# Hybrid decoder step: output projection and second norm interleaved with the MLP of the group before

## The chip, the cores and the metric

The kernel runs on all 8 cores of one Trainium2 chip, two dies of four cores. Every core runs the same program on its own share of the batch. The metric is device time in microseconds of the slowest core. TensorE (PE) does the matmuls, VectorE (DVE) and ScalarE (ACT) the elementwise work, GpSimd (POOL) a little at the start, and SyncE (SP) issues every DMA from one in-order queue.

## The reference, cut to what matters

```python
def _layer(h, ...):
    xn = _rmsnorm(h, ln_mix)
    zq, zf, zi, zg, sq, sk, sv = _split(xn @ w_in)
    o_hg, S_new = _hgrn2(zq, zf, zi, zg, lb, hg_norm, S0)     # linear recurrence, 4 heads of 128
    o_swa = _swa_prompt(q, k, v, sinks)                       # window 128, 8 query heads, 2 kv heads
    h = h + jnp.concatenate([o_hg, o_swa], axis=-1) @ w_out
    u = _rmsnorm(h, ln_mlp) @ w_up
    h = h + jnp.square(jax.nn.relu(u)) @ w_down
    return h, S_new, k_buf, v_buf
y = _rmsnorm(h, ln_final)
```

The model width is 1024, the MLP width 4096. Each core has one prompt sequence of 4096 tokens and 16 decoding sequences of 8 tokens each (128 tokens, the "sample"), with their recurrent states and key/value caches.

## The kernel before, in words

The prompt's 4096 tokens are 32 tiles of 128 tokens, worked in 8 groups of four. For a group the tile of activations is kept transposed, 8 blocks of 128 features by 512 tokens: xnT (normed x), omT (mixer output), hnT (normed h), aT (MLP activation). The residual stream XR has 8 slots of one token tile, so two groups.

The weights are 24 chunks of 1024 x 512. Chunks 0 to 5 are the input projection, 6 and 7 the output projection, 8 to 15 w_up, 16 to 23 w_down. A ring of five slots (s_wr) holds them in bf16. At its first use a chunk comes as fp32 in four quarters to s_stg, is cast by ScalarE and VectorE in turns (L337 to L350) and stored to wbf in HBM; from then on it is read from there. `w_release` frees a slot and issues the next chunk's load; `w_use` puts the pending casts into the engines' queues. Ten chunks are cast before and during the sample's own mixer, the other 14 after it.

Work is written as generators that yield after each step, and the order in which a step is emitted is its order in each engine's in-order queue:

- `head12_steps`: first norm of four tiles (`norm_pre`: statistics on ScalarE, L457 to L461, scale on VectorE to s_xnb, L468; `norm_post`: 8 transposes, L475, and a copy, L477), then the input projection (`fm_mm` L486, `tm_mm` L493), the gates of the recurrence (L540 to L562), and keys and values.
- `p3_tile_steps`: the mixer of one tile in nine steps. Recurrence: L611, L619, L663 to L669, norm L637. Window attention: scores L716, exp L720, mask multiply L723, values L742 and denominators L743, and `swa_finish` (four adds L694, a reciprocal L699, a multiply into omT L707).
- `p45`: for each tile two output matmul groups (L898, 8 matmuls each), the add into XR (L902), `norm_pre`, and, two tiles late, `norm_post` into hnT.
- `mlp_steps`: four rounds of 8 up groups (L486 on hnT; relu L928, square into aT L931) and 8 down groups (L939, add into XR L943). One group is 8 matmuls.
- `p8`: final norm (L457, L960) and the store of y.

Each phase allocates one of 8 PSUM banks per group, in the order in which banks came free. A wait is set by whole buffers: any write to hnT must be done before a matmul that reads any part of it.

The main loop for group g loads x for g+1, runs `p45(g)` by itself, then takes one step of `mlp_steps(g)` and one of the front half of g+1 (`head12_steps`, then the mixer) in turns until both are done, then `p8(g)`. Ahead of the loop the sample's `p45` and MLP are taken in turns with the front half of group 0; this is where the 14 chunks are cast.

The softmax here doesn't subtract the row's maximum and nothing guards it: scores larger than these inputs give would overflow.

## Time and profile before

| | us |
|---|---|
| median of 3 runs (2219.98 to 2221.53) | 2221.41 |
| span of the profiled execution, slowest core | 2217.1 |
| spans of the eight cores | 2200.3 to 2217.1 |
| TensorE busy | 1667.9 (75%) |
| ScalarE busy | 931.1 (42%) |
| VectorE busy | 864.2 (39%) |

Of the profiled execution the profile gives the span alone, from the first to the last instruction of the slowest core; its own time as the runs are timed is not given. The median of the runs is 4.3 us over that span. A busy TensorE is not TensorE at full rate: its granted clock is shown beside it, and matmuls at half the clock count as busy for twice as long. Line numbers are those of the kernel before.

### The profile page before, as it was taken

What the parts mean: (1) busy time and instruction counts of PE and PEld (TensorE: products, weight loads), DVE (VectorE), ACT (ScalarE), POOL (GpSimd) and SP (SyncE); (2) the same over time, 40 slices, a digit from 0 to 9 for tenths busy, and PEclk for the clock granted to TensorE, in tenths of its full rate; (3) what the DMA queues carried; (4) which work ended last, traced back from release to release, by engine and by line L of the source; (5) the groups of instructions that cost most, each with busy time, mean ns of one, the idle gap of its engine ahead of it and who ended that gap; (6) DMA issues with size and microseconds to landing.
All of it is one profiled execution on the core that took longest, in us unless ns stands there. A gap on an engine that the chain in (4) does not pass through costs nothing.

```text
span 2217.1 us, 26417 instructions; the slowest of 8 cores (2200.3 to 2217.1 us)
## 1 busy us (share of the span) xinstructions
PE 1667.9 (75%) x8533; PEld 773.3 (35%) x8533; DVE 864.2 (39%) x1438; ACT 931.1 (42%) x1861; POOL 28.6 (1%) x59
## 2 busy tenths in 40 slices
PE   0301354345999699969996999699969996999797
PEld 0201232212443244334433443344334443443343
DVE  1113413144245624561356235523652355235412
ACT  1312334242446344544454454444444444444433
POOL 2001000000000000000000000000000000000000
PEclk9755586766999899989998999899989998999899
DMA  7774476760242434343424342434334333442332
GB/s 193 229 223 142 142 247 233 272 226 32 102 171 99 168 106 161 114 152 125 147 108 152 133 152 98 149 133 152 114 133 152 135 113 133 152 155 95 128 143 76
DMA packets 77767, 326.66 MB, mean 147 GB/s; under 512 B 7584, under 2 KB 29088, under 8 KB 49952
## 3 DMA queue, kind: packets, MB, share of 16 engines
q1 hardware_dynamic: 77632, 324.97, 42.6%
q8 instruction: 71, 1.16, 0.2%
q14 instruction: 64, 0.52, 0.1%
HBM read 277.76 MB, written 49.15 MB: 147 GB/s over the span
## 4 chain that ended last, share of the span: by engine, by line
PE 59%; DMA 11%; DVE 10%; ACT 9%; issue 6%; SPq 2%; POOL 0%; ACTq 0%; DVEq 0%; POOLq 0%
PE pb L486 27%; PE pb L939 19%; DMA s_stg<-wall 9%; PE pb L898 4%; PE pb L493 3%; DVE U L699 3%; ACT s_junk L457 3%; SPq L103 2%; PE pb L742 2%; DMA XR<-st 2%; DVE XR L902 2%; PE pb L716 1%; ACT s_rl L928 1%; PE pb L743 1%; ACT U L720 1%
## 5 line engine op out<-in xcount | busy, mean ns | idle before, releaser
L939 PE MATMUL pb<-s_wr,s_aT 128*128 128x512 bf16 x2112 | 497.3, 382 | 88.3 <-ACT s_aT L931 29.1
L486 PE MATMUL pb<-s_hnT,s_wr 128*128 128x512 bf16 (+1 forms) x2304 | 507.1, 369 | 17.5 <-ACT s_rl L928 8.0
L943 DVE TENSOR_TENSOR XR<-pb,XR 128x512 f32<-128x512 f32 x264 | 182.2, 690 | 557.0 <-PE pb L939 555.2
L939 PEld LDWEIGHTS pb<-s_wr,s_aT 128*128 128x128 bf16 x2112 | 199.8, 98 | 333.4 <-issue 119.3
L486 PEld LDWEIGHTS pb<-s_hnT,s_wr 128*128 128x128 bf16 x2304 | 214.7, 100 | 264.0 <-issue 49.9
L486 PE MATMUL pb<-s_xnT,s_wr 128*128 128x512 bf16 (+1 forms) x1224 | 274.2, 373 | 19.8 <-ACT U L521 9.6
L928 ACT ACTIVATE s_rl<-pb 128x512 bf16<-128x512 f32 (+1 forms) x288 | 160.2, 556 | 198.1 <-PE pb L486 197.9
L931 ACT ACTIVATE s_aT<-s_rl 128x512 bf16<-128x512 bf16 (+1 forms) x288 | 171.6, 596 | 27.0 <-ACT s_rl L928 0.7
L898 PE MATMUL pb<-s_wr,s_omT 128*128 128x512 bf16 x528 | 141.5, 435 | 52.0 <-DVE s_omT L707 46.0
L486 PEld LDWEIGHTS pb<-s_xnT,s_wr 128*128 128x128 bf16 x1224 | 120.3, 103 | 148.8 <-issue 25.3
L457 ACT ACTIVATE s_junk<-XR 128x1024 bf16<-128x1024 f32 x99 | 103.8, 1048 | 160.5 <-DVE XR L902 134.0
L475 PE MATMUL pb<-s_ident,s_xnb 128*128 128x128 bf16 x528 | 49.2, 255 | 149.5 <-DVE s_xnb L468 149.3
L699 DVE RECIPROCAL U<-U 128x512 f32<-128x512 f32 x33 | 110.6, 3353 | 3.4
L720 ACT ACTIVATE U<-pb 128x512 bf16<-128x512 f32 x128 | 75.6, 591 | 85.5 <-PE pb L716 85.5
L493 PE MATMUL pb<-s_wr,s_xnT 128*128 128x256 bf16 (+1 forms) x528 | 100.1, 334 | 9.5 <-ACT U L532 9.5
L898 PEld LDWEIGHTS pb<-s_wr,s_omT 128*128 128x128 bf16 x528 | 56.5, 109 | 136.1 <-issue 92.1
L475 PEld LDWEIGHTS pb<-s_ident,s_xnb 128*128 128x128 bf16 x528 | 41.2, 115 | 162.3 <-issue 156.3
L468 DVE TENSOR_SCALAR s_xnb<-XR,s_rs 128x1024 bf16<-128x1024 f32 x66 | 49.6, 752 | 115.6 <-ACT s_rs L461 115.6
L742 PE MATMUL pb<-U,s_vS_all 128*64 128x512 bf16 x126 | 54.1, 429 | 43.4 <-DVE U L723 43.3
L621 ACT COPY U<-pb 128x512 bf16<-128x512 bf16 x33 | 19.2, 582 | 141.0 <-PE pb L619 141.0
L723 DVE TENSOR_TENSOR U<-U,s_swm_cur 128x512 bf16<-128x512 bf16 x64 | 27.2, 426 | 117.9 <-ACT U L720 117.9
L493 PEld LDWEIGHTS pb<-s_wr,s_xnT 128*128 128x128 bf16 x528 | 52.3, 100 | 51.4 <-issue 13.7
(140 smaller groups left out, 1349.0 us busy)
## 6 DMA issues: line engine op xcount, KB each, us to landing
s_wr<-wbf SPq DMA_DIRECT2D x192, 1024.0 KB, 4.9
s_stg<-wall SPq DMA_DIRECT2D x96, 512.0 KB, 8.7
wbf<-s_wr SPq DMA_DIRECT2D x24, 1024.0 KB, 4.8
XR<-x SPq DMA_DIRECT2D x32, 512.0 KB, 6.0
y<-XR SPq DMA_DIRECT2D x32, 512.0 KB, 4.1
XR<-st SPq DMA_DIRECT2D x16, 256.0 KB, 3.2
ss<-XR SPq DMA_DIRECT2D x16, 256.0 KB, 2.6
XR<-ck SPq DMA_DIRECT2D x4, 256.0 KB, 4.1
```

The costliest lines, as they stand in the source:

```text
L457: P.op("act", lambda e: e.activation(out=junk[:, :], in_=src[:, :], func=AF.Square, accum_out=ssq[:, 0:1]), reads=[src], writes=[ssq, junk])
L475: P.op("pe", [lambda e, k=k: e.transpose(bkb[:, k * 128:(k + 1) * 128], xb[:, k * 128:(k + 1) * 128], C.ident[:, :]) for k in range(8)], r ...
L486: P.op("pe", [lambda e, k=k: e.matmul(bk[0:ncols, 0:TB], lhsT=W[:, k, col0:col0 + ncols], rhs=srcT[:, k, 0:TB], start=(k == 0), stop=(k == ...
L493: P.op("pe", [lambda e, k=k: e.matmul(bk[:, 0:ncols], lhsT=srcT[:, k, j * 128:(j + 1) * 128], rhs=W[:, k, 0:ncols], start=(k == 0), stop=( ...
L699: P.op("dve", lambda e: e.reciprocal(out=B.rden[:, :], in_=B.dsum[:, :]), reads=[B.dsum], writes=[B.rden])
L720: P.op("act", lambda e: e.activation(out=pt[:, :], in_=bkS[:, :], func=AF.Exp, scale=0.125), reads=[bkS], writes=[pt])
L742: P.op("pe", [lambda e: e.matmul(swO[rows, :], lhsT=vS_all[:, ks, rows], rhs=pt[:, :], start=first, stop=last), lambda e: e.matmul(swD[row ...
L898: P.op("pe", [lambda e, k=k, W=W, bk=bk: e.matmul(bk[:, :], lhsT=omT[:, k, j * 128:(j + 1) * 128], rhs=W[:, k, :], start=(k == 0), stop=(k ...
L928: P.op("act", lambda e, bk=bk, rl=rl: e.activation(out=rl[:, 0:TB], in_=bk[:, 0:TB], func=AF.Relu), reads=[bk], writes=[rl])
L931: P.op("act", lambda e, fl=fl, rl=rl: e.activation(out=aT[:, fl, 0:TB], in_=rl[:, 0:TB], func=AF.Square), reads=[rl], writes=[aT])
L939: P.op("pe", [lambda e, f=f, W=W, j=j, bk=bk: e.matmul(bk[:, :], lhsT=aT[:, f, j * 128:(j + 1) * 128], rhs=W[:, f, :], start=(f == 0), sto ...
L943: P.op("dve", lambda e, nh=nh, bk=bk, xs_=xs_: e.tensor_tensor(out=xs_[:, nh * 512:(nh + 1) * 512], in0=bk[:, :], in1=xs_[:, nh * 512:(nh ...
```

## The change

The output projection and the second norm leave their own phase. `p45` goes. `back_steps` takes the mixer of a group's tiles and, after the third and the sixth step of tile j, one output group of tile j-1 each; the transposes of the second norm follow behind the next output group. All of it belongs to the front half, which runs beside the MLP of the group before, so hnT gets a second buffer (taken from the space of the DMA scratch). x for group g+2 is loaded when the MLP of g ends. `p8` of a tile follows its last down group.

The two halves no longer take turns one by one. Each step yields a weight; a first build sums them, and `interleave` keeps the two sums in proportion, after 6 steps of the MLP alone. In the front half the chunks come in the order 2, 0, 1, 3, 4, 5, and each gate step stands ahead of one group of chunk 3. The transposed tiles are tracked by token tile (xnT, hnT, omT) or by feature row (aT), and a down group is issued in three parts (6, 1 and 1 matmuls), each with its own wait.

```diff
+W_DENSE = 0.25
+W_ATT = 1.2
+W_OUT = 0.6
+W_WAIT = 3.0
+PACE = 1.04
+LEAD = 6
...
-    nc = bass.Bass("TRN2", target_bir_lowering=False)
+    nc = bass.Bass("TRN2", target_bir_lowering=False, dynamic_dma_scratch_size=1024)
...
-    xnT = sb("xnT", [8, 512], BF16)
-    hnT = sb("hnT", [8, 512], BF16)
+    class Cols:
+        __slots__ = ("ap", "t")
...
+            if cut == "cols":
+                self.t = [Buf(self.ap[:, :, j * 128:(j + 1) * 128]) for j in range(n // 128)]
+            else:
+                self.t = [Buf(self.ap[:, k, :]) for k in range(8)]
...
+    xnT = Cols("xnT", 512, "cols")
+    hnTs = [Cols("hnT%d" % i, 512, "cols") for i in range(2)]
...
-    omT = sb("omT", [8, 512], BF16)
-    aT = sb("aT", [8, 512], BF16)
+    omT = Cols("omT", 512, "cols")
+    aT = Cols("aT", 512, "rows")
...
-             reads=[W, srcT], writes=[bk])
+             reads=[W] + srcT.t[0:TB // 128], writes=[bk])
...
+            xbs.append(norm_pre(slots[j]))
+            if j < 2:
+                yield W_WAIT
+            if j >= 1:
+                norm_post(xbs[j - 1], xnT, j - 1)
+                yield W_OUT
+        yield W_OUT
+        norm_post(xbs[nt - 1], xnT, nt - 1)
+        yield W_DENSE
+        W, u = w_use(2)
...
+        for cid, dst in ((0, B.qtT), (1, B.sgT)):
+            W, u = w_use(cid)
...
         W, u = w_use(3)
         for g in range(4):
+            gate(g)
             bk = fm_mm(W, g * 128, xnT, TB)
...
+    def back_steps(B, tiles, slots, hn):
+        pend = []
+
+        def post():
+            if pend:
+                xb0, j0 = pend.pop(0)
+                norm_post(xb0, hn, j0)
+
+        def out_tile(Ws, j):
+            for nh, W in enumerate(Ws):
+                out_mm(W, nh, j, slots[j])
+                if nh == 0:
+                    post()
+                yield W_OUT
+            pend.append((norm_pre(slots[j]), j))
+
+        Ws = None
+        prev = iter(())
         for j, n in enumerate(tiles):
-            for _ in p3_tile_steps(B, j, n):
-                yield
-        if tiles[-1] == NT - 1:
-            for h in range(4):
-                final_toks.append(P.dma(sp_d[h], S[h].ap, reads=[S[h]], sem="spo"))
+            for i, w in enumerate(p3_tile_steps(B, j, n)):
+                yield w
+                if j > 0 and i in (2, 5):
+                    if Ws is None:
+                        (W6, u6), (W7, u7) = w_use(6), w_use(7)
+                        Ws = (W6, W7)
+                    if i == 2:
+                        prev = out_tile(Ws, j - 1)
+                    w = next(prev, None)
+                    if w is not None:
+                        yield w
+            for w in prev:
+                yield w
+            if j == len(tiles) - 1:
+                yield W_WAIT
+            if n == NT - 1:
+                for h in range(4):
+                    final_toks.append(P.dma(sp_d[h], S[h].ap, reads=[S[h]], sem="spo"))
+        for w in out_tile(Ws, len(tiles) - 1):
+            yield w
+        w_release(u6)
+        w_release(u7)
+        while pend:
+            yield W_WAIT
+            post()
...
-    def p45(B, slots):
...
+    def out_mm(W, nh, j, xs_):
+        bk = psum()
+        P.op("pe", [lambda e, k=k: e.matmul(bk[:, :], lhsT=omT[:, k, j * 128:(j + 1) * 128], rhs=W[:, k, :],
+                                            start=(k == 0), stop=(k == 7)) for k in range(8)],
+             reads=[omT.t[j], W], writes=[bk])
+        P.op("dve", lambda e: e.tensor_tensor(out=xs_[:, nh * 512:(nh + 1) * 512], in0=bk[:, :],
+                                              in1=xs_[:, nh * 512:(nh + 1) * 512], op=ALU.add), reads=[bk], writes=[xs_])
+        pfree(bk)
...
+                    for fa, fb in ((0, 6), (6, 7), (7, 8)):
+                        P.op("pe", [lambda e, f=f: e.matmul(bk[:, :], lhsT=aT[:, f, j * 128:(j + 1) * 128], rhs=W[:, f, :],
+                                                            start=(f == 0), stop=(f == 7)) for f in range(fa, fb)],
+                             reads=aT.t[fa:fb] + [W], writes=[bk])
...
+                    if q == 3 and nh == 1:
+                        p8(slots[j], ydst[j * 128:(j + 1) * 128, :])
+                    yield 1.0
...
+    def interleave(key, genA, genB, lead):
+        done = {"a": 0.0, "b": 0.0}
+        total = (weights or {}).get(key, {"a": 1.0, "b": 1.0})
+        ok = {"a": True, "b": True}
+
+        def step(which, gen):
+            w = next(gen, None)
+            if w is None:
+                ok[which] = False
+            else:
+                done[which] += w
+
+        for _ in range(lead):
+            step("a", genA)
+        a0 = done["a"]
+        while ok["a"] or ok["b"]:
+            fa = (done["a"] - a0) / max(1e-6, total["a"] - a0)
+            fb = done["b"] / max(1e-6, total["b"])
+            if ok["b"] and (fb <= fa * PACE or not ok["a"]):
+                step("b", genB)
+            else:
+                step("a", genA)
+        wsum[key] = done
...
+            p45_sample(Bs, xsmp, hnTs[1])
+            yield 1.0
+            for w in mlp_steps(Bs, [xsmp], hnTs[1], ys_d):
+                yield w
+
+        def front(g):
+            slots = [xload[n] for n in gtiles(g)]
+            return chain(head12_steps(Bp, gtiles(g), slots, False), back_steps(Bp, gtiles(g), slots, hnTs[g % 2]))
+
+        interleave("s", sample_tail(), front(0), 0)
...
+        for n in gtiles(1):
+            load_x(n)
...
+            genA = mlp_steps(Bp, [xload[n] for n in gtiles(g)], hnTs[g % 2], y_d[g * G * 128:(g + 1) * G * 128, :])
+            interleave(g, genA, front(g + 1) if g + 1 < NG else iter(()), LEAD if g + 1 < NG else 0)
+            if g + 2 < NG:
...
-            xb_last = p45(Bp, slots)
-            genA = mlp_steps(Bp, slots, xb_last)
-            if g + 1 < NG:
-                nslots = [xload[n] for n in gtiles(g + 1)]
-                genB = chain(head12_steps(Bp, gtiles(g + 1), nslots, False), head3_steps(Bp, gtiles(g + 1)))
-                interleave(genA, genB)
-            else:
-                drain(genA)
-            p8(slots, y_d[g * G * 128:(g + 1) * G * 128, :])
...
+    _, _, steps = build_program()
+    _, order, _ = build_program(weights=steps)
+    nc, _, _ = build_program(worder=order, weights=steps)
```

TensorE at the end of a group's mixer, before (L716, L742, L743: attention; L898: output projection; L475: transposes of the norms; L486 on s_hnT: the next MLP):

```order
L716 MATMUL pb<-U,s_kT_all 128x512
L742 MATMUL pb<-U,s_vS_all 64x512
L743 MATMUL pb<-U,s_ones 64x512
L898 MATMUL pb<-s_wr,s_omT 128x512 x48
L475 MATMUL pb<-s_ident,s_xnb 128x128 x8
L898 MATMUL pb<-s_wr,s_omT 128x512 x16
L475 MATMUL pb<-s_ident,s_xnb 128x128 x40
L486 MATMUL pb<-s_hnT,s_wr 128x512 x8
```

The same place in the changed kernel (L754, L755: attention; L506: up groups; L979: down groups; L941: output projection; L495: transposes):

```order
L754 MATMUL pb<-U,s_vS_all 64x512
L755 MATMUL pb<-U,s_ones 64x512
L506 MATMUL pb<-s_hnT,s_wr 128x512 x16
L979 MATMUL pb<-s_wr,s_aT 128x512 x24
L941 MATMUL pb<-s_wr,s_omT 128x512 x8
L495 MATMUL pb<-s_ident,s_xnb 128x128 x8
L941 MATMUL pb<-s_wr,s_omT 128x512 x8
L979 MATMUL pb<-s_wr,s_aT 128x512 x24
L495 MATMUL pb<-s_ident,s_xnb 128x128 x8
L979 MATMUL pb<-s_wr,s_aT 128x512 x16
L506 MATMUL pb<-s_hnT,s_wr 128x512 x64
```

The block of 64 output matmuls is gone; its last two groups stand between down groups of the preceding MLP, and 64 up matmuls of the next group follow without front work.

ScalarE late in the weight stream, before (L337, L347: casts of a chunk; L584: keys; L928, L931: relu and square of the sample's MLP):

```order
L337 ACTIVATE s_wr<-s_stg,s_lnmlp 128x512 x4
L584 CAST s_kT_all<-pb 128x512
L928 ACTIVATE s_rl<-pb 128x128
L931 ACTIVATE s_aT<-s_rl 128x128
L337 ACTIVATE s_wr<-s_stg,s_lnmlp 128x512 x4
L347 CAST s_wr<-s_stg 128x1024 x4
```

The changed kernel in the same stream (L367, L357: casts; L687, L693, L639: recurrence; L732: exp of attention; L967, L970: relu and square):

```order
L367 CAST s_wr<-s_stg 128x1024 x2
L967 ACTIVATE s_rl<-pb 128x128
L970 ACTIVATE s_aT<-s_rl 128x128
L687 ACTIVATE U<-pb,U 128x128 x4
L693 CAST s_S_bf<-Sst 128x512
L639 ACTIVATE U<-pb 128x512
L967 ACTIVATE s_rl<-pb 128x128
L970 ACTIVATE s_aT<-s_rl 128x128
L732 ACTIVATE U<-pb 128x512
```

Steps of the mixer stand between the casts of one chunk and the next, where before the casts followed each other closely.

## Rows read from the trace of the kernel before

**Rows 1.** Windows of core 7: busy us (instructions), granted clock, DMA share, GB/s.

```profile
core 7: us, PE busy (x) PEld busy (x) DVE busy (x) ACT busy (x) POOL busy (x), PEclk, DMA share, GB/s
...
260.00:470.00 210.00, 91.16 (x579) 51.55 (x580) 54.83 (x100) 80.07 (x169) 0.00 (x0) 0.71 0.71 252
470.00:532.00 62.00, 27.63 (x108) 9.39 (x106) 34.47 (x56) 20.80 (x43) 0.00 (x0) 0.56 0.25 90
532.00:561.00 29.00, 21.57 (x114) 10.91 (x115) 13.54 (x22) 11.24 (x28) 0.00 (x0) 0.79 0.20 73
561.00:744.00 183.00, 172.83 (x858) 77.18 (x856) 73.23 (x123) 84.65 (x156) 0.00 (x0) 0.99 0.35 127
560.00:2087.00 1527.00, 1365.65 (x6792) 616.39 (x6789) 674.04 (x1062) 707.20 (x1383) 0.00 (x0) 0.95 0.38 134
```

**Rows 2.** Timeline of TensorE (start, us): attention of group 0 alone, first MLP matmul.

```profile
489.07 0.61 PE L611 MATMUL pb<-U 128*128 128x128 bf16 x4
...
507.83 0.61 PE L611 MATMUL pb<-U 128*128 128x128 bf16 x4
...
560.53 2.69 PE L486 MATMUL pb<-s_hnT,s_wr 128*128 128x512 bf16 x8 [0.19 <-DVE s_hnT L477]
```

**Rows 3.** Timelines of TensorE, VectorE and the DMA queue in the last group.

```profile
2087.41 15.91 PE L486 MATMUL pb<-s_hnT,s_wr 128*128 128x512 bf16 x64 [1.18 <-DVE s_hnT L477]
...
2193.36 13.97 PE L939 MATMUL pb<-s_wr,s_aT 128*128 128x512 bf16 x64 [1.67 <-ACT s_aT L931]
2208.11 4.86 DVE L960 SCALAR_TENSOR_TENSOR XR<-XR,s_rs,s_gfin 128x1024 f32<-128x1024 f32 x4
2209.47 3.91 SPq L103 DMA_DIRECT2D y<-XR  x4
```

**Rows 4.** TensorE waits, 560 to 2087 us: sum, times, longest, in us.

```profile
PE pb L475 <- DVE s_xnb L468: 60.1, 21, 6.2
PE pb L898 <- DVE s_omT L707: 40.2, 7, 5.8
PE pb L742 <- DVE U L723: 33.1, 28, 1.4
PE pb L939 <- DVE s_omT L707: 14.1, 7, 2.0
PE pb L939 <- ACT s_aT L931: 11.7, 7, 1.7
```

**Rows 5.** Timeline of TensorE at a group boundary: start, us, [idle <-releaser].

```profile
962.62 0.60 PE L742 MATMUL pb<-U,s_vS_all 128*64 128x512 bf16 x1 [1.37 <-DVE U L723]
...
969.39 13.38 PE L898 MATMUL pb<-s_wr,s_omT 128*128 128x512 bf16 x48 [5.74 <-DVE s_omT L707]
...
994.54 2.74 PE L475 MATMUL pb<-s_ident,s_xnb 128*128 128x128 bf16 x24 [5.90 <-DVE s_xnb L468]
997.46 2.68 PE L486 MATMUL pb<-s_hnT,s_wr 128*128 128x512 bf16 x8 [0.19 <-DVE s_hnT L477]
```

**Rows 6.** Timeline of VectorE at the end of one attention tile.

```profile
489.25 1.13 DVE L694 TENSOR_SCALAR U<-pb,s_esinkT 128x128 f32<-128x128 f32 x4 [1.29 <-PE pb L743]
...
493.94 0.69 DVE L707 TENSOR_TENSOR s_omT<-pb,U 128x512 bf16<-128x512 f32 x1
```

**Rows 7.** DMA issues by line: KB each, median us from issue to landing.

```profile
XR<-x SPq DMA_DIRECT2D x32, 512.0 KB, 6.0
y<-XR SPq DMA_DIRECT2D x32, 512.0 KB, 4.1
```

**Rows 8.** Timeline of the DMA queue in the weight stream.

```profile
422.05 3.08 SPq L103 DMA_DIRECT2D s_stg<-wall  x4
434.46 0.33 SPq L103 DMA_DIRECT2D wbf<-s_wr  x1
```

**Rows 9.** Timeline of ScalarE in the same stretch.

```profile
416.60 1.34 ACT L337 ACTIVATE s_wr<-s_stg,s_lnmlp 128x512 bf16<-128x512 f32 x2 [5.39 <-DMA s_stg<-wall]
```

**Rows 10.** Window of core 0 in a dense stretch.

```profile
790.00:870.00 80.00, 80.00 (x393) 37.88 (x392) 26.98 (x41) 29.91 (x53) 0.00 (x0) 1.00 0.43 152
```

More of the change, by code:

```diff
@@ L511, in head12_steps @@
+        yield W_OUT
+        norm_post(xbs[nt - 1], xnT, nt - 1)
+        yield W_DENSE
+        W, u = w_use(2)
+        sm = B.smask_s if sample else C.smask
         for h in range(4):
             bk = fm_mm(W, h * 128, xnT, TB)
-            P.op("act", lambda e, h=h, bk=bk: e.activation(out=B.qtT[:, h, :], in_=bk[:, 0:TB], func=AF.Silu),
-                 reads=[bk], writes=[B.qtT])
+            P.op("act", lambda e, h=h, bk=bk: e.activation(out=B.sg4[h][:, :], in_=bk[:, 0:TB], func=AF.Tanh, scale=0.5),
+                 reads=[bk], writes=[B.sg4[h]])
@@ L515, in head12_steps @@
             pfree(bk)
-            yield
+            yield W_DENSE
         w_release(u)
-        W, u = w_use(1)
-        for h in range(4):
-            bk = fm_mm(W, h * 128, xnT, TB)
-            P.op("act", lambda e, h=h, bk=bk: e.activation(out=B.sgT[:, h, :], in_=bk[:, 0:TB], func=AF.Silu),
-                 reads=[bk], writes=[B.sgT])
-            pfree(bk)
-            yield
-        w_release(u)
-        W, u = w_use(2)
-        sm = B.smask_s if sample else C.smask
-        for hp in range(1):
-            for hh in range(4):
-                h = hh
+        for cid, dst in ((0, B.qtT), (1, B.sgT)):
+            W, u = w_use(cid)
+            for h in range(4):
@@ L571, in head12_steps @@
             pfree(bk)
-            yield
+            yield W_DENSE
         w_release(u)
@@ L888, in p3_sample_body, with p45_sample, mlp_steps @@
         yield
-    def p45(B, slots):
-        nt = B.TB // 128
+    def out_mm(W, nh, j, xs_):
[6 more added lines that the diff above has]
+        pfree(bk)
+    def p45_sample(B, slot, hn):
         W6, u6 = w_use(6)
         W7, u7 = w_use(7)
-        pend = []
-        for j in range(nt):
-            for nh, W in enumerate((W6, W7)):
-                bk = psum()
-                P.op("pe", [lambda e, k=k, W=W, bk=bk: e.matmul(bk[:, :], lhsT=omT[:, k, j * 128:(j + 1) * 128],
-                                                                rhs=W[:, k, :], start=(k == 0), stop=(k == 7))
-                            for k in range(8)], reads=[omT, W], writes=[bk])
-                xs_ = slots[j]
-                P.op("dve", lambda e, nh=nh, bk=bk, xs_=xs_: e.tensor_tensor(
-                    out=xs_[:, nh * 512:(nh + 1) * 512], in0=bk[:, :], in1=xs_[:, nh * 512:(nh + 1) * 512], op=ALU.add),
-                     reads=[bk], writes=[xs_])
-                pfree(bk)
-            xb = norm_pre(slots[j])
-            pend.append((xb, j))
-            if len(pend) > 2:
-                xb0, j0 = pend.pop(0)
-                norm_post(xb0, hnT, j0)
+        for nh, W in enumerate((W6, W7)):
+            out_mm(W, nh, 0, slot)
         w_release(u6)
         w_release(u7)
-        return pend
-    def mlp_steps(B, slots, xb_last):
+        norm_post(norm_pre(slot), hn, 0)
+    def mlp_steps(B, slots, hn, ydst):
         TB = B.TB
         nt = TB // 128
-        for xb0, j0 in xb_last:
-            norm_post(xb0, hnT, j0)
-            yield
         for q in range(4):
```

168 lines of the change are left out of this document (64 added, 104 removed).

## The prediction

> **What bounds the kernel now.** First the windows over the whole run [rows 1]: between 561 and 744 us TensorE is busy for 172.8 of 183 us at a granted clock of 0.99, while VectorE and ScalarE have under half of the time and the DMA share is 0.35. The stretches around it are poor: 470 to 532 keeps TensorE busy 27.6 of 62 us. Then the timeline, to cut the span at the first MLP matmul of each group. Group 0 has it at 560.53 [rows 2], group 7 at 2087.41 [rows 3]. So the 2217.1 us are 560.5 (start) + 1526.9 (seven periods of 218.1) + 129.7 (last group).
>
> The list of TensorE's waits prices the periods [rows 4]. TensorE is idle 1527.00 - 1365.65 = 161 us [rows 1], 23.0 a period, and the list names 159.2 of it: 100.3 on the xnb tiles of the norms and on the omT tile ahead of the output projection, 33.1 on the mask multiply of attention, 14.1 on a PSUM bank that VectorE frees late, 11.7 on aT. The boundary's timeline adds a second loss [rows 5]. 48 matmuls of L898 took 13.38 us behind an idle time of 5.74. At full rate 64 took 13.97 [rows 3], 0.216 each and 0.17 of drain, so 48 should take 10.5: 2.9 lost. The 24 transposes (a quarter of the columns each, so 1.5 us) took 2.74, the first 8 MLP matmuls 2.68 instead of 1.9, and the last attention pair 0.4 too long. That is 5.3 us of half clock a period. What is left, 218.1 - 23.0 - 5.3 = 189.8 us, is TensorE's work at full rate. TensorE bounds the periods.
>
> **The seven periods.** No matmul goes or comes. The 64 of L898 and the transposes of the second norm move under the MLP before. The waits of 100.3/7 = 14.3 us a period end. On xnb: the longest is 6.2 [rows 4], and now three down groups stand between an output matmul and its transposes, 3 x 1.73 = 5.2 us, while the final norm's work, which came in one block just before, is spread tile by tile. On omT: five groups, 8.6 us, stand between the last attention pair and its output matmul, against 5.4 for the end of a tile on VectorE, from 489.25 to 494.63 [rows 6]. With no idle time near 5 us the half clock should go too. What is late next, by the order of the changed kernel:
> - A bank freed by L707. VectorE takes the down group's add first and then the 5.4 us; the waiting group stands 5.9 us behind. This is the wait of 2.0 that occurs once a period now [rows 4]; the order has it behind two of four tiles: 4.0.
> - The mask multiply: now 33.1/7 = 4.7 a period. The output groups give cover to three of four tiles; one pair without cover (1.4, as the 1.37 in [rows 5]) and one behind the statistics (1.0) stay: 2.4.
> - x. It was loaded a whole group ahead of its output projection; now it is issued when the group ends and is wanted after 6 lead steps, 6 x 1.73 = 10.4 us. The last y of the kernel leaves the queue at 2209.47 + 3.91 = 2213.4, 6.0 behind the last matmul (2207.3) [rows 3]. Per-tile y stores make this earlier at best; x then lands 6.0 later [rows 7], 12 us at most, and the slot's y store takes 4.1 beside it. ScalarE waits in order, and the relus of two groups and with them aT stand behind it: up to 2 us at the first down group, and 1.1 at one transpose. I take 3.1.
> - The three-part wait on aT. A down group begins after six of eight rows; the 11.7/7 = 1.7 goes into the line above.
> Sum 9.5, so 199.3 a period and 1395 for seven. Below: 190, if all of these hide. Above: 213, if the old 23 us of waits come back under other names and only the clock is won.
>
> **The start.** This is the least certain term, for the gain is not where it seems. From 260 on the fp32 weights of the MLP are loaded and cast: 12.4 us from one chunk's first load to its store [rows 8], with ScalarE standing still at the head of its queue until the data is there (5.4 of it here) [rows 9]. 14 chunks, 174 us. Attention of tiles 2 to 4 trails it with 18.8 us a tile (489.07 to 507.83) [rows 2], then 29 us of output projection and norm [rows 1]. Pacing by weights now spreads all four tiles over the stream. But ScalarE and VectorE are in order and the casts stand right behind each load, so attention's steps do not run under the load; only what TensorE has already issued does, and the next load needs the slot that TensorE frees behind those steps. My sum, from 260: +9 as one more cast pair stands ahead of the sample's attention and holds the cache loads back; 15 for the four norms; 24 for the twelve dense groups, which now come before the first chunk of the stream (12 x 1.73, and 3 of slow clock); 174 for the 14 chunks; 8 for the gates; 35 for attention; 5 for the rest. That makes 530 for the first MLP matmul of group 0. The 35 is about half of the four tiles' 75 us: the steps ahead of the last matmul on each of five up-projection chunks, 7 us each. Ends: 0 (all hidden, 495) and 75 (nothing hidden, 570).
>
> **The last group.** 8 x 64 matmuls x 0.216 = 110.8; aT waits fall from 4 x 1.67 to some 0.4 each, 1.6; from the last matmul to the end now 9.8, less 1.2 because a tile's final scale no longer queues behind three others (four take 4.86) [rows 3]: 8.6. Together 121.
>
> **Sum.** 530 + 1395 + 121 = 2046 of span. The profiled span of before stands 4.3 under the median of the runs, 2221.4; with that, 2050, 7.7% less.
>
> **A rule against it.** The longest dense stretch of a core now is about 180 us, and the clock in it is 0.99 on core 7 [rows 1] and 1.00 on core 0 of the other die [rows 10]: the upper of the two levels, 2.4 GHz. The changed kernel asks for this over 1500 us on eight cores. The Trainium skill (TensorE: Matmul & The Clock Gate, Part 1: The HAM clock gate) says that a current limiter takes a whole die to 13/16 of the clock once three of its cores run dense matmuls. By that rule a period would be 187 x 16/13 + 12 = 242, and the kernel some 2380. The trace disagrees with it: all eight cores run this program side by side, and neither die is below 0.99 in a dense stretch.
>
> **Rivals.**
> - The clock gives way under the longer load (slower). Place: every period. For it: none has run this dense this long. Against: [rows 10], and no decay towards the end of a stretch. Some 187 us of matmul time a period stretch; if a quarter of them ran at the lower level a period would be 187 x 1.25 + 12 = 246, in all 2380. It decides from (2217 - 530 - 121)/7 = 224 a period on, a mean clock of about 0.88 in the dense part. 3 in 100.
> - The waits move and do not go: in-order ScalarE and VectorE carry statistics, relus and attention in one mix, TensorE keeps 23 us idle. For it: three of my four terms are such waits. Against: VectorE and ScalarE work 674 and 707 of 1527 us [rows 1]. 530 + 7 x 213 + 121 + 4 = 2146. 8 in 100.
> - The start gains nothing, because attention is serial with the casts and the stream starts later: 570 to 590. For it: [rows 9]. 580 + 1395 + 121 + 4 = 2100. 12 in 100.
> - Everything hides: 505 and 194 a period, 505 + 1358 + 121 + 4 = 1988. 9 in 100.
> - The change does not do what it says: the order shows the output matmuls between MLP groups in every group, so only if the numbers of the pacing left a tail of attention. 1 in 100, near 2200.
>
> **How the numbers follow.** The forecast has 67 in 100. The range 2000 to 2110 takes in the case of the poor start and leaves out the others, about 20 in 100. Slower has the clock and 1 for what I do not see. The measurement tells 0.2%, 4 us, from no change; same has 1.
>
> **What would show it.** Periods of 195 to 205 us between first MLP matmuls; no TensorE wait on xnb or omT over 2 us; the clock at 0.98 or more from group 0 on; waits of 2.0 on L707's bank about twice a period; the first MLP matmul of group 0 at 510 to 550; a first down group that waits for aT with ScalarE behind a DMA of x. Wrong I would be with a period over 210, a clock under 0.95 in the dense part, or a start beyond 570.

## The result: 2.6 per cent faster, where 7.7 were forecast

The changed kernel takes 2150.9 us in the profiled execution; its ratio to the kernel before is 0.974, 95% interval 0.968 to 0.980, so about 2163 us beside 2221. Both figures lie above the range. In some executions one or both dies ran at a lower clock (three of six of the changed kernel), and the ratios leave these out on both sides, while the medians hold all (2186.5 for the changed kernel). In what follows a ratio is always to the kernel before, timed beside it, and a gain in us is a difference of two ratios times 2221; a gain in per cent is of the kernel before unless said otherwise.

**Profile after.** Windows of core 1, the slowest, as in [rows 1]:

```profile
core 1: us, PE busy (x) PEld busy (x) DVE busy (x) ACT busy (x) POOL busy (x), PEclk, DMA share, GB/s
260.00:470.00 210.00, 118.34 (x674) 61.74 (x672) 80.67 (x142) 91.82 (x193) 0.00 (x0) 0.74 0.63 222
...
509.00:2022.00 1513.00, 1383.07 (x6805) 619.64 (x6803) 669.90 (x1062) 709.10 (x1390) 0.00 (x0) 0.97 0.38 137
```

The timeline of TensorE gives the cuts, the first MLP matmul of groups 0, 1 and 7:

```profile
508.93 13.98 PE L506 MATMUL pb<-s_hnT,s_wr 128*128 128x512 bf16 x64
...
718.11 15.66 PE L506 MATMUL pb<-s_hnT,s_wr 128*128 128x512 bf16 x64 [3.28 <-DVE s_hnT L497]
...
2022.40 3.05 PE L506 MATMUL pb<-s_hnT,s_wr 128*128 128x512 bf16 x7 [3.28 <-DVE s_hnT L497]
```

So 2149.8 = 508.9 (start) + 1513.5 (seven periods of 216.2) + 127.4 (last group). Against the forecast the start is 21 us better, a period 16.9 us worse (118 in seven) and the last group 6 us worse.

The waits of TensorE between 509 and 2022 us, in the columns of [rows 4]:

```profile
PE pb L979 <- ACT s_aT L970: 27.8, 14, 4.2
PE pb L506 <- DVE s_hnT L497: 20.6, 6, 3.6
PE pb L754 <- DVE U L735: 14.8, 14, 1.7
PE pb L506 <- DVE s_omT L719: 14.6, 7, 2.1
PE pb L513 <- DVE U L581: 14.5, 7, 2.1
PE pb L979 <- DVE s_omT L719: 14.4, 7, 2.4
PE pb L495 <- DVE s_xnb L488: 8.1, 7, 1.2
PE pb L649 <- ACT U L639: 6.2, 7, 0.9
PE pb L675 <- ACT s_aT L970: 4.5, 7, 0.8
```

The list ends just ahead of group 7; the wait of 3.28 us for hnT there belongs to the seventh period too, so hnT has 23.9 us in seven. The waits on xnb and on omT ahead of the output projection, 100 us in [rows 4], are down to 8 us, and those on the mask from 33 to 15, but some 80 us have come under other names. A period is 197.6 us of busy TensorE (1383.07/7) and 18.6 idle. The busy part is 7.8 more than the 189.8 at full rate: that much is slow clock, by the forecast's own figure for full rate, and more than the 5.3 of before. The mean granted clock rose all the same (0.95 to 0.97), since it counts idle time as well, and less of the time at half clock is now idle.

Where the two largest waits arise, the timeline of a group's end shows: VectorE, ScalarE, TensorE and the DMA queue, first column the start.

```profile
710.10 1.06 ACT L477 ACTIVATE s_junk<-XR 128x1024 bf16<-128x1024 f32 x1 [1.55 <-DVE XR L983]
712.10 1.28 DVE L1000 SCALAR_TENSOR_TENSOR XR<-XR,s_rs,s_gfin 128x1024 f32<-128x1024 f32 x1 [2.10 <-ACT s_rs L481]
713.30 0.68 DVE L983 TENSOR_TENSOR XR<-pb,XR 128x512 f32<-128x512 f32 x1
...
716.07 1.29 DVE L1000 SCALAR_TENSOR_TENSOR XR<-XR,s_rs,s_gfin 128x1024 f32<-128x1024 f32 x1 [2.09 <-ACT s_rs L481]
717.28 0.69 DVE L497 COPY s_hnT<-pb 128x1024 bf16<-128x1024 bf16 x1
...
724.64 1.28 DVE L1000 SCALAR_TENSOR_TENSOR XR<-XR,s_rs,s_gfin 128x1024 f32<-128x1024 f32 x1 [2.10 <-ACT s_rs L481]
...
726.48 0.33 SPq L109 DMA_DIRECT2D s_wr<-wbf  x1
726.92 3.69 SPq L109 DMA_DIRECT2D XR<-x  x4
...
735.55 1.06 ACT L477 ACTIVATE s_junk<-XR 128x1024 bf16<-128x1024 f32 x1 [3.83 <-DMA XR<-x]
...
738.74 0.38 PE L979 MATMUL pb<-s_wr,s_aT 128*128 128x512 bf16 x1 [3.67 <-ACT s_aT L970]
...
739.94 6.78 PE L979 MATMUL pb<-s_wr,s_aT 128*128 128x512 bf16 x17 [0.83 <-ACT s_aT L970]
```

Read it by VectorE. The add of a tile's last down step (L983) is followed by ScalarE's statistics of that tile, and those by the final scale (L1000). The scale stands in VectorE's queue ahead of the next tile's add, so VectorE stands idle for 2.1 us in each tile and the next statistics cannot begin. A tile takes 4.0 us (712.10 to 716.07) where TensorE delivers one in 1.8. Two things stand behind this chain. The copy of the last hnT tile (717.28) is queued behind the second scale, and TensorE waits 3.28 us for it. The last scale ends at 725.9, and the x loads into the same buffers are issued at 726.9, 8.8 us after the group began; x lands at 735.5, ScalarE stands at the head of its queue for it, the relus are queued behind, and TensorE waits 3.67 + 0.83 us for aT.

### The profile page after: what moved, and what is told of

Its sections match the earlier page's. It is cut to its first block, busy times and chain, and to the rows that moved or that the text cites. A ratio compares the mean times of both kernels' runs of the same rounds, so it can differ in the third digit from the quotient of the medians.

```text
span 2149.8 us, 26519 instructions; the slowest of 8 cores (2123.1 to 2149.8 us)
## 1 busy us (share of the span) xinstructions
PE 1686.1 (78%) x8533; PEld 778.1 (36%) x8533; DVE 860.4 (40%) x1438; ACT 929.2 (43%) x1861; POOL 28.8 (1%) x59
## 4 chain that ended last, share of the span: by engine, by line
PE 52%; DMA 13%; DVE 13%; ACT 11%; issue 8%; SPq 2%; POOL 0%; ACTq 0%; DVEq 0%; POOLq 0%
PE pb L506 22%; PE pb L979 16%; DMA s_stg<-wall 7%; PE pb L941 5%; ACT s_junk L477 3%; DMA XR<-x 3%; DVE U L711 3%; SPq L109 2%; DVE U L558 2%; PE pb L754 2%; DMA XR<-st 2%; ACT s_rl L967 1%; DVE XR L983 1%; PE pb L495 1%; PE pb L728 1%
## 5 line engine op out<-in xcount | busy, mean ns | idle before, releaser
L506 PE MATMUL pb<-s_hnT,s_wr 128*128 128x512 bf16 (+1 forms) x2304 | 516.6, 378 | 45.3 <-DVE s_hnT L497 24.8
L979 PE MATMUL pb<-s_wr,s_aT 128*128 128x512 bf16 x2112 | 512.6, 393 | 44.0 <-ACT s_aT L970 29.0
L506 PEld LDWEIGHTS pb<-s_hnT,s_wr 128*128 128x128 bf16 x2304 | 219.4, 103 | 304.6 <-issue 101.5
L983 DVE TENSOR_TENSOR XR<-pb,XR 128x512 f32<-128x512 f32 x264 | 181.2, 689 | 354.2 <-PE pb L979 353.3
L979 PEld LDWEIGHTS pb<-s_wr,s_aT 128*128 128x128 bf16 x2112 | 203.8, 100 | 305.5 <-issue 100.4
L506 PE MATMUL pb<-s_xnT,s_wr 128*128 128x512 bf16 (+1 forms) x1224 | 257.3, 372 | 17.9 <-ACT U L545 8.9
L967 ACT ACTIVATE s_rl<-pb 128x512 bf16<-128x512 f32 (+1 forms) x288 | 160.1, 556 | 205.1 <-PE pb L506 204.9
L970 ACT ACTIVATE s_aT<-s_rl 128x512 bf16<-128x512 bf16 (+1 forms) x288 | 171.0, 594 | 26.8 <-ACT s_rl L967 0.4
L506 PEld LDWEIGHTS pb<-s_xnT,s_wr 128*128 128x128 bf16 x1224 | 119.7, 103 | 150.0 <-issue 25.4
L941 PE MATMUL pb<-s_wr,s_omT 128*128 128x512 bf16 x528 | 133.8, 400 | 11.6 <-DVE s_omT L713 5.6
L732 ACT ACTIVATE U<-pb 128x512 bf16<-128x512 f32 x128 | 75.4, 589 | 115.6 <-PE pb L728 114.8
L495 PE MATMUL pb<-s_ident,s_xnb 128*128 128x128 bf16 x528 | 43.5, 230 | 87.9 <-DVE s_xnb L488 87.9
L545 ACT ACTIVATE U<-pb 128x512 bf16<-128x512 f32 (+1 forms) x72 | 40.4, 561 | 97.3 <-PE pb L506 96.8
L941 PEld LDWEIGHTS pb<-s_wr,s_omT 128*128 128x128 bf16 x528 | 53.1, 102 | 76.4 <-issue 21.8
L754 PE MATMUL pb<-U,s_vS_all 128*64 128x512 bf16 x126 | 51.8, 411 | 34.5 <-DVE U L735 34.5
L944 DVE TENSOR_TENSOR XR<-pb,XR 128x512 f32<-128x512 f32 x66 | 45.6, 691 | 80.4 <-PE pb L941 80.3
L495 PEld LDWEIGHTS pb<-s_ident,s_xnb 128*128 128x128 bf16 x528 | 36.7, 103 | 103.5 <-issue 91.7
```

Of the source, the lines that this page charges most:

```text
L495: P.op("pe", [lambda e, k=k: e.transpose(bkb[:, k * 128:(k + 1) * 128], xb[:, k * 128:(k + 1) * 128], C.ident[:, :]) for k in range(8)], r ...
L506: P.op("pe", [lambda e, k=k: e.matmul(bk[0:ncols, 0:TB], lhsT=W[:, k, col0:col0 + ncols], rhs=srcT[:, k, 0:TB], start=(k == 0), stop=(k == ...
L732: P.op("act", lambda e: e.activation(out=pt[:, :], in_=bkS[:, :], func=AF.Exp, scale=0.125), reads=[bkS], writes=[pt])
L754: P.op("pe", [lambda e: e.matmul(swO[rows, :], lhsT=vS_all[:, ks, rows], rhs=pt[:, :], start=first, stop=last), lambda e: e.matmul(swD[row ...
L941: P.op("pe", [lambda e, k=k: e.matmul(bk[:, :], lhsT=omT[:, k, j * 128:(j + 1) * 128], rhs=W[:, k, :], start=(k == 0), stop=(k == 7)) for ...
L967: P.op("act", lambda e, bk=bk, rl=rl: e.activation(out=rl[:, 0:TB], in_=bk[:, 0:TB], func=AF.Relu), reads=[bk], writes=[rl])
```

## The experiments

| kernel | median, us | ratio, 95% interval | period, us (core) |
|---|---|---|---|
| changed kernel | 2186.5 | 0.974 (0.968 to 0.980) | 216.2 (1) |
| late scale | 2104.1 | 0.944 (0.941 to 0.947) | 210.6 (2) |
| twelve x buffers | 2119.0 | 0.949 (0.944 to 0.953) | 210.7 (7) |
| both | 2078.8 | 0.934 (0.932 to 0.937) | 206.1 (3) |
| finish in one block | 2100.5 | 0.943 (0.940 to 0.946) | 210.4 (7) |
| whole-buffer waits | 2199.1 | 0.985 (0.981 to 0.990) | 219.1 (5) |
| back half alone | 2243.9 | 1.008 (1.005 to 1.010) | 225.1 (3) |
| back half alone, finish in one block | 2189.7 | 0.983 (0.979 to 0.987) | 218.2 (7) |
| both, room around the gates | 2046.2 | 0.919 (0.917 to 0.922) | 202.4 (7) |
| both, bank copied out | 2071.7 | 0.929 (0.926 to 0.932) | 205.8 (7) |
| both, room, bank copied out | 2054.3 | 0.926 (0.923 to 0.929) | 202.7 (2) |
| the same, finish in one block in place of the late scale | 2045.9 | 0.922 (0.918 to 0.926) | 202.8 (1) |
| room around the gates alone | 2124.8 | 0.954 (0.951 to 0.958) | 212.3 (0) |

**Late scale.** The final scale of a tile is issued behind the next tile's add:

```diff
                     if q == 3 and nh == 1:
-                        p8(slots[j], ydst[j * 128:(j + 1) * 128, :])
+                        late.append((norm_stats(slots[j]), slots[j], ydst[j * 128:(j + 1) * 128, :]))
+                        if j:
+                            p8(*late.pop(0))
                     yield 1.0
                 w_release(u)
+        p8(*late.pop(0))
```

> Edit: in the last down step of a group the final scale (VectorE) of tile j and its y store are issued behind the add of tile j+1, not straight behind the statistics of tile j; no instruction more or less. Theory (the serial finish): VectorE, in order, holds the next tile's add until ScalarE's statistics of this tile are done, so a tile takes 4.0 us where TensorE gives one every 1.8; this makes the copy of the last hnT tile late (TensorE waits 3.6 us at each group's start and then runs 1.7 us slow), and makes the last y store, behind which the x loads of the same buffers wait, some 7 us late (ScalarE waits 4.4 us for x, TensorE 5.0 us for aT, then about 2 us at half clock). All of it should go: 12 us a period, seven periods, 2065 us (2055 to 2090); x lands some 7 us earlier and no wait for aT over 1 us is left at the second down step. Rival A (x is late by itself, its transfer of 9 us being the cause): only the start wait goes, 5 us a period, 2113 us. Rival B (the gaps move on): 2135 us or more.

A boundary of this kernel (core 2):

```profile
925.05 13.98 PE L506 MATMUL pb<-s_hnT,s_wr 128*128 128x512 bf16 x64
...
930.64 7.74 SPq L109 DMA_DIRECT2D XR<-x  x4
...
938.67 1.06 ACT L477 ACTIVATE s_junk<-XR 128x1024 bf16<-128x1024 f32 x1 [1.68 <-DMA XR<-x]
...
941.85 0.38 PE L980 MATMUL pb<-s_wr,s_aT 128*128 128x512 bf16 x1 [1.53 <-ACT s_aT L971]
```

The wait at the group's start is gone, and with it the slow matmuls (13.98 for 64, not 15.66). x is issued 5.6 us after the group's start, not 8.8, but takes 8 us to land. A wait for aT of 2.4 us in place of 4.5 is left in this period, and over the seven periods (510 to 1984 us) most of these waits stay, 20.7 us of 27.8:

```profile
PE pb L980 <- ACT s_aT L971: 20.7, 14, 3.5
```

3.0 per cent are won (0.974 to 0.944), 67 us for 84 expected. The profiled executions are less far apart, 46 us (2149.8 and 2103.4 of span): 5.6 us a period and 8 in the last group. The expectation that no wait for aT over 1 us is left failed. By the total the result lies between the theory and rival A; by the places it is rival A, for what went is the wait at the start of the group and the slow matmuls behind it, some 5 us a period.

**Twelve x buffers.** The staging buffers of the float weights become x buffers 8 to 11, and x is issued in the middle of the MLP two groups before:

```diff
+    xres += [Buf(t_.ap.rearrange("p a b -> p (a b)")) for t_ in stg32]
 ...
-            s = xres[n % NXS]
+            s = xres[n % 12]
 ...
+            if q == 1 and hook is not None:
+                hook()
```

> Edit: twelve x buffers where there were eight (the four more are the staging buffers of the float weights, unused after the first pass), and the x loads of a group issued in the middle of the MLP two groups before, so that none waits for a y store and each is there about 200 us ahead of its use. The serial finish stays. Theory: only the part that runs through x goes: the 5.0 us of waits for aT and the 2 us at half clock behind them, 7 us a period, 2102 us (2090 to 2115); the 3.6 us wait for the hnT copy at the start of a group stays. Rival A (transfer of x is the cause of both waits): the same figure for this run, but then the late scale alone gives no more than 2113. Rival B (the gaps move on to the next late instruction): 2135 us or more.

Waits of core 7, 509 to 2000 us:

```profile
PE pb L507 <- DVE s_hnT L498: 23.9, 7, 3.6
...
PE pb L982 <- ACT s_aT L971: 7.5, 8, 2.3
```

The wait for aT falls from 27.8 to 7.5 and that for hnT stays, as the theory said; 56 us won for 49 expected.

> Edit: the late scale and the twelve x buffers together. Theory (the serial finish is the root of both waits): no better than the late scale alone, since with it x is early enough: 2065 us (2055 to 2090), within 0.3 per cent of that run. Rival A: 2065 here against 2113 for the late scale alone. Rival B: the gain of each alone is small and theirs together too: 2130 us.

The late scale alone stands at 0.944, both at 0.934. So the theory's claim that the serial finish alone is the root of both waits falls: x is late by the finish and by its own landing time together. At this kernel's boundary (core 3) no wait for hnT is left, and the waits for aT are down to 7.3 us in seven periods (513 to 1955 us):

```profile
925.86 13.98 PE L507 MATMUL pb<-s_hnT,s_wr 128*128 128x512 bf16 x64
...
942.08 3.83 PE L983 MATMUL pb<-s_wr,s_aT 128*128 128x512 bf16 x17 [0.73 <-ACT s_aT L972]
...
PE pb L983 <- ACT s_aT L972: 7.3, 8, 2.1
```

**Finish in one block.** The four calls of p8 stand behind the last down step again, as before the change:

```diff
-                    if q == 3 and nh == 1:
-                        p8(slots[j], ydst[j * 128:(j + 1) * 128, :])
 ...
+        for j in range(nt):
+            p8(slots[j], ydst[j * 128:(j + 1) * 128, :])
```

> Edit: the final statistics, scale and y store of all four tiles are issued in one block behind the last down step, as in the kernel before, in place of tile by tile. Theory: the wait for the hnT copy at the start of a group goes (5 us a period with the slow clock behind it), while the last y store stays as late as it is (four statistics of 1.8 us behind the last add end about where they end now), so the waits for aT stay; and ScalarE's 7 us of statistics now stand ahead of the first relu of the next group, so that TensorE may run out of banks: between 2113 and 2150 us, the middle 2130. Rival A and B give the same range; what it tells apart is whether finishing tile by tile, taken by itself, gains or loses time: I expect it to lose.

It gains 3.1 per cent, as much as the late scale, and 2100.5 us lies under the range that was expected (2113 to 2150). So finishing tile by tile, which the change brought, costs some 70 us by the ratios and 50 between the profiled spans. In the block VectorE does four scales back to back (4.86 us) and no statistics wait between them. TensorE has no wait for hnT in the seven periods, and those for aT stay nearly whole (core 7, 505 to 1978 us), both as expected:

```profile
PE pb L979 <- ACT s_aT L970: 25.3, 14, 3.5
```

**Whole-buffer waits.** One wait per buffer again:

```diff
-                self.t = [Buf(self.ap[:, :, j * 128:(j + 1) * 128]) for j in range(n // 128)]
 ...
+            self.t = [Buf(self.ap)] * 8
```

> Edit, on the changed kernel as it stands (its median is 2186.5, its profiled run 2150.9 us): xnT, hnT, omT and aT are each one buffer again for the waits, no longer cut by token tile or row; the order of all instructions is the same. Theory: the cut is worth what the first down step of each of the four quarters would wait for the last square (1.2 us of relu and square less what the front's steps cover) and what the output projection of a tile would wait for the next tile's omT, some 2 to 5 us a period: 2165 to 2190 us where the changed kernel shows 2151. Rival: the front's steps between cover all of it, and the cut is worth nothing (2145 to 2158).

```profile
PE pb L976 <- ACT s_aT L967: 49.6, 26, 5.5
```

In its seven periods (core 5, 517 to 2052 us) the waits for aT are 49.6 us where they were 27.8, all others as they were: 22 us, and the ratio moves by 0.0115, some 25 us. Waits by tile and by row are worth about 1 per cent, by way of aT; the two intervals only just part, so the size is rough.

**Back half alone.** Output projection and second norm in a block behind the MLP, first with the tile-wise finish, then with the finish in a block:

```diff
-                if j > 0 and i in (2, 5):
+                if False:
 ...
+    def tail_steps(B, tiles, slots, hn):
+        pend = []
+        (W6, u6), (W7, u7) = w_use(6), w_use(7)
+        for j in range(len(tiles)):
+            for nh, W in enumerate((W6, W7)):
+                out_mm(W, nh, j, slots[j])
+            pend.append((norm_pre(slots[j]), j))
 ...
```

> Edit, on the changed kernel as it stands: output projection and second norm of a group are issued in one block behind the MLP of the group before, as in the kernel before the change; the cut buffers, the paced turns, the tile-wise finish and the second hnT buffer stay. Theory: the idle time at the group boundary is back (8.6 us for xnb, 5.7 for omT, 5.3 at half clock in each period of the kernel before), while the block of 14 us hides what the tile-wise finish costs (5.3 us at the start of the group, 7 us behind the late x): 7 us a period slower than the changed kernel, 2200 us (2170 to 2225), and the first MLP matmul of group 0 some 20 us later, at 525 us. Rival: interleaving is worth little, since what it fills the finish takes: 2150.

> Edit, on the changed kernel: output projection and second norm in one block behind the MLP (as in the run that gave 2243.9 us) and the final statistics, scales and y stores in one block too. This is the order of the kernel before at the group's end; the second hnT buffer, the cut waits, the paced turns and the moved gates of the change are all there. Theory: against the run with the block finish and the interleaved back half (2100.5 us) the boundary waits of the kernel before come back, 14.3 us idle and 5.3 at half clock a period, less the 5 us of waits for aT behind the late x, which is now early: 14.6 a period, 102 us, 2203 us (2185 to 2225); so the rest of the change is worth 1 per cent or less of the kernel before, and interleaving nearly all. In this kernel the tile-wise finish costs 30 to 50 us as it does in the interleaved one. Rival: the 2243.9 us had nothing to do with the finish: 2235 to 2250 again.

The first is slower than the kernel before, by 0.7 per cent, and 2243.9 us lies above the range expected (2170 to 2225): that the block of output projection hides the tile-wise finish was wrong. Its xnb waits (core 3, 548 to 2123 us), one of the longest of them, and the waits of the second (core 7, 529 to 2056 us), each in seven periods:

```profile
PE pb L495 <- DVE s_xnb L488: 117.7, 28, 10.6
...
1432.36 1.01 PE L495 MATMUL pb<-s_ident,s_xnb 128*128 128x128 bf16 x8 [10.22 <-DVE s_xnb L488]
```

```profile
PE pb L495 <- DVE s_xnb L488: 74.6, 28, 4.2
PE pb L513 <- DVE U L581: 21.0, 7, 3.0
```

In the first the serial finish stands ahead of the second norm on VectorE; the two kernels differ by 2.5 per cent, 55 us, a little more than the 30 to 50 expected, and the second came out at 2189.7 us for 2203, inside its range. With the changed kernel (0.974) and its block finish (0.943) they complete a square of two edits: interleaving gains 4.0 per cent with the block finish (0.983 to 0.943) and 3.4 with the tile-wise one, the tile-wise finish loses 3.1 and 2.5. And the kernel with the block finish and the back half alone has the periods of the kernel before, 218.2; its whole gain is in the start, 529 us for 560 on core 7, and in the last group, 123.6 for 129.7. So the periods owe their gain to the interleaving. What the rest of the change does inside them comes out at nothing: the mask waits are down from 33.1 to 3.4 us in seven periods, but the moved gates bring the bank wait behind L581 (21.0, none in [rows 4]), and the xnb waits are 74.6 for 60.1.

**Room around the gates, and the bank copied out**, each on the kernel with both edits:

```diff
-            yield W_DENSE
+            yield W_GATE
```

(after each qsT group; W_GATE = 0.9, W_DENSE = 0.25)

```diff
+        if not sample:
+            P.op("act", lambda e: e.copy(out=B.oc[:, :], in_=bkO[:, :]), reads=[bkO], writes=[B.oc])
+            pfree(bkO)
```

> Edit, on the kernel with late scale and twelve x buffers (2078.8 us): the four steps that hold a gate and a qsT group count 0.9 in the pacing where they counted 0.25, so that more MLP steps stand between them. Theory: VectorE's backlog of the four gates, for which the next v matmul waits 2.1 us for a bank, goes, with up to 1.7 us of slow clock behind it: 15 to 27 us in seven periods, 2057 us (2050 to 2066). Rival: the wait moves to another bank or to the norm at the group end, where there are now fewer MLP steps: 2075 to 2085.

> Edit, on the kernel with late scale and twelve x buffers (2078.8 us): ScalarE copies the attention output out of its bank (bf16, 128x512, one more instruction of 0.58 us a tile), and VectorE's reciprocal and multiply no longer hold that bank. Theory: the two waits of TensorE for a bank freed by the omT multiply (2.1 and 2.0 us a period) go, with up to 2 us of slow clock behind them: 2043 us (2036 to 2055). Rival: the banks are handed out in turn, and the next in line is freed no earlier: 2070 us or more.

The room gives 1.5 per cent, 33 us for 22 expected; it has the lowest ratio of the study, 8.1 per cent under the kernel before. Its edit moved the whole pacing and not one wait: in seven periods (core 7) the bank wait for L581 (14.5 us) is gone, and with it the 14.4 of the down groups on L719's bank and 11.4 of the 14.8 of the attention mask, while two others are new, 23.0 for the recurrence's masked scores (L628) and 8.1 for the first norm's xnT. So the gain belongs to the sum of these and not to L581 alone. The copy gives 0.5 per cent, 12 us for 36, and 2071.7 us is what its rival said (2070 or more): its two waits have gone, and another stands in their place, that of TensorE for the masked scores (core 7, seven periods):

```profile
PE pb L677 <- DVE U L628: 24.4, 14, 2.1
```

> Edit: late scale, twelve x buffers, room around the gates (2046.2 us with these three) and the attention output copied out of its bank, all four. Theory: what is left of the waits for the omT multiply (2.0 us a period) goes with the slow clock behind it, as the copy alone gave 7 us: 2037 us (2030 to 2043). Rival: the copy gained its 7 us from waits that the room around the gates has already taken away: 2046, within 0.2 per cent.

> Edit: as the run with all four parts, but the four final statistics, scales and y stores in one block behind the last down step in place of the late scale. Theory: with twelve x buffers nothing waits for the y stores, so the only question is what VectorE and ScalarE have in order ahead of the next group; the block puts 7 us of statistics on ScalarE ahead of the first relu of the group, which the late scale spreads, so it is slower by up to 3 us a period: 2037 to 2058. Rival: since the block by itself gained as much as the late scale by itself (2100.5 and 2104.1 us), it does so here too: within 0.2 per cent of the run with all four.

With the room there, the copy does not help (2054.3 us for 2037 expected; 0.926 for 0.919, and the intervals just part): the wait for the masked scores is 38.1 us against 23.0 without it. And block or late scale make no difference that the intervals tell (0.922 and 0.926); the rival's 0.2 per cent is finer than they are.

> Edit, on the changed kernel as it stands (0.974 of the kernel before in its undisturbed runs, 2163 us): only the room around the four gates (0.9 in the pacing for 0.25). Theory: its gain of 32 us is independent of the late finish, since it lies in the middle of the period: 2131 us (2120 to 2140). Rival: it depends on x being early, because the steps of the front that it stretches begin later here: 2145 to 2163.

2.0 per cent (0.974 to 0.954), 43 us for 32 expected, and 2124.8 us is inside the range: the gain does not hang on the finish. That it is larger here than with both edits (33) is not shown, since the interval of the changed kernel alone is 13 us wide to either side.

## Why the prediction was wrong, step by step

**The last group and the finish: the step that failed.** "Per-tile y stores make this earlier at best", and "a tile's final scale no longer queues behind three others". The instructions are the same, but their order on VectorE makes each scale wait for ScalarE and each add wait for the scale. I read off that the four scales of the block take 4.86 us [rows 3] and asked what a scale waits for; I did not ask what is queued behind a waiting scale. In the last group the tail from the last matmul to the end is 14.2 us (2135.6 to 2149.8) where I had 8.6 and the block had 9.8:

```profile
2121.40 14.18 PE L979 MATMUL pb<-s_wr,s_aT 128*128 128x512 bf16 x64
...
2142.53 0.68 DVE L983 TENSOR_TENSOR XR<-pb,XR 128x512 f32<-128x512 f32 x1
```

That is nearly all of the 6 us in which the last group was longer; with the late scale the last group takes 119.6 us. In the periods the same chain gives the hnT wait (3.4 a period) that no term of mine had, the 1.7 at half clock behind it, and part of the x term. The two edits that take the chain away give back 67 and 70 us by the ratios and 46 and 50 between the profiled spans, of the 104 us by which the forecast of the span was too low. That this step failed is shown; the rest of the miss lies in the two steps on waits and on the clock below.

**x.** Forecast: landed by 12 us at most, 3.1 us of waits. Measured: issued 8.8 and landed 17.4 us after the group's start; waits for aT 4.6 a period with L675's. Of the delay of 5.4 us half is the finish and half the landing, 9.1 us in the median for 6.0 in [rows 7]:

```profile
XR<-x SPq DMA_DIRECT2D x32, 512.0 KB, 9.1
y<-XR SPq DMA_DIRECT2D x32, 512.0 KB, 2.9
```

The mechanism was named and its sign in the profile was right (a first down group that waits for aT with ScalarE behind a DMA of x); only the size was not. Of the wait the finish is the smaller part, for the late scale took only 7 us of 27.8 away and the earlier load 20. At the start of group 0, with no finish of a prompt group ahead of it, x is issued after 5.4 us and TensorE still waits 1.75 and 0.83 us for aT. The 6.0 was the median of loads at another place of the period, behind four y stores as well, but 10 us ahead of the next weight chunks:

```profile
970.42 3.91 SPq L103 DMA_DIRECT2D y<-XR  x4
974.66 4.49 SPq L103 DMA_DIRECT2D XR<-x  x4
985.03 2.05 SPq L103 DMA_DIRECT2D s_wr<-wbf  x2
```

In the changed kernel a chunk (1024 KB) is issued 0.4 us ahead of x and two more 3.9 us behind (726.48 and 730.78 us). With twelve x buffers no y store stands ahead of x, a chunk does, and x lands in 8.5 us in the median. So the longer landing does not need the y stores; that the weight chunks cause it is likely, but no run moved them alone.

**Other waits.** The bank behind L719: 4.0 forecast, 4.1 measured. The mask: 2.4 and 2.1. What I had not seen: the bank that L581 frees late, since the four gates now stand between the qsT groups (2.1), the last xnb tile (1.2) and the norm's squares (0.9). Idle time in all 18.6 for 9.5, which is 64 us of the 118 in seven periods. The room around the gates, which moved the first together with other waits, gave 33 to 43 us.

**The clock: a term put at nothing.** "With no idle time near 5 us the half clock should go too". It did not: 7.8 us a period, 55 us of the 118, the largest single term of the miss (the 1.7 behind the hnT wait is part of it). It comes behind shorter idle times. 64 matmuls take 15.66 behind 3.28 us of idle time and 13.98 behind none; 17 take 6.78 behind the two waits for aT shown above (3.67 and 0.83), 5.15 at the next boundary (4.20 and 0.83) and, in the kernel with both edits, 3.83. A wait of 2.0 was followed by it too, but not each:

```profile
831.30 3.54 PE L979 MATMUL pb<-s_wr,s_aT 128*128 128x512 bf16 x8 [2.01 <-DVE s_omT L719]
```

```profile
801.63 2.78 PE L513 MATMUL pb<-s_wr,s_xnT 128*128 128x256 bf16 x24 [2.07 <-DVE U L581]
```

8 matmuls of 512 columns in 3.54 us are at half rate; 24 of 256 columns in 2.78 are at full rate, behind an idle time as long. What tells the two apart is open. So waits taken away give more than their own length: with both edits a period is 206.1, 10.1 less, of which some 6 are idle time and some 4 clock.

The sentence of mine on the current limiter stands: in the dense part both kernels have the upper clock.

```profile
754.00:796.00 42.00, 42.00 (x196) 19.05 (x195) 12.25 (x19) 16.73 (x29) 0.00 (x0) 1.00 0.38 127
```

By the rule of the Trainium skill (TensorE: Matmul & The Clock Gate, Part 1: The HAM clock gate) a stretch like this would run at 13/16 of the clock on all eight cores. The trace disagrees: between 754 and 796 us the granted clock is 0.96 to 1.00 on every core of both dies, with TensorE busy for 39.4 to 42.0 of the 42 us. The forecast's estimate by that rule, 2380 us, was also added up wrong: 530 + 7 x 242 + 121 + 4 is 2349.

**The start: right in direction, too dear by 21.** The stream of the 14 chunks in the DMA queue's timeline: its first load, the first store and the last. The kernel before:

```profile
265.04 3.92 SPq L103 DMA_DIRECT2D s_stg<-wall  x4
279.26 0.33 SPq L103 DMA_DIRECT2D wbf<-s_wr  x1
...
458.64 0.33 SPq L103 DMA_DIRECT2D wbf<-s_wr  x1
```

The changed kernel:

```profile
301.43 2.12 SPq L109 DMA_DIRECT2D s_stg<-wall  x4
313.84 0.33 SPq L109 DMA_DIRECT2D wbf<-s_wr  x1
...
495.14 0.33 SPq L109 DMA_DIRECT2D wbf<-s_wr  x1
```

The stream starts at 301, where the forecast's terms ahead of it add up to 308; it takes 193.7 us, for 174 + 35; its end is followed by 13.8 us, forecast 13. That makes 6.6 + 15.3 - 0.8 = 21. The stream of the kernel before took 193.6 us from first load to last store, so two terms were off and partly made up for each other: the 174, taken from the one chunk of [rows 8] (12.4 us, where the mean of the stream is 13.8), was 20 too low, and attention beside the stream cost nothing that can be told, where "half of the four tiles' 75 us" had 35. The rival of the poor start (570 to 590) is refuted by the 508.9.

**The sum.** 2046 - 21 + 118 + 6 = 2149.8 to the rounding. The rival closest in time is "the waits move and do not go" (2146, 8 in 100), with another mechanism in part: it kept 23 us of idle time a period and won the clock, while idle time fell by a fifth, to 18.6, and it was the clock that was not won. That its 2146 is so near the 2149.8 is luck: its period is 213 for 216.2 and its start 530 for 508.9. Of the signs, no wait on xnb or on omT ahead of an output projection over 2 us came true (1.2 the longest), "the clock at 0.98 or more" did not (0.97), and "wrong with a period over 210" was met.

## What to carry to other kernels

When a block of work is cut up and spread over the steps that feed it, look at each queue in order, at what stands behind the instruction that waits for another engine; here the cure was to issue one tile's scale behind the next tile's add, and doing all in a block was as good. A buffer that is reused across the boundary ties the next load to the very end of that chain: give the load another buffer before shortening the chain. And price an idle time of TensorE of 2 us and more at up to 1.8 times its length (2.01 and then 1.65 lost at half clock here), both when it goes and when a new one comes.

## What was not expected of the hardware

- Idle times of 2.0 and 3.3 us were followed by some 1.7 us lost at half clock, one of 4.5 in two parts by 2.95 and one of 5.0 by 1.3, and another of 2.07 by none, where before I had charged it only to waits of 5 to 6 us.
- The same 512 KB load of x landed in 6.0 us (median) in the kernel before, right behind four y stores, and in 9.1 in the changed kernel, where the load of a weight chunk stands beside it; the y stores landed in 4.1 and 2.9.
- The float weight stream kept its 13.8 us a chunk with the attention of four tiles beside it, and TensorE's busy time between 260 and 470 us rose from 91 to 118 us.
